# Front of a hybrid decoder layer: three square roots instead of two, GpSimd normalizes the second half, six PSUM banks, other queues for three loads

## What is computed

```python
h = rmsnorm(x, ln1_g)               # xf * rsqrt(mean(xf * xf) + 1e-6) * g
x = x + hybrid_mixer(h, w_in, ...)  # h @ w_in, 8 stick-breaking heads, 4 linear-attention heads, @ w_out
h = rmsnorm(x, ln2_g)
x = x + hierarchical_moe(h, ...)    # 4 groups of 8 experts, top 2 of one group
return rmsnorm(x, ln_f_g)
```

## Time and profile before

| | us |
|---|---|
| median of three runs (lowest, highest) | 1315.86 (1309.72, 1317.32) |
| profiled execution: span from first to last instruction | 1320.3 |
| TensorE matmuls busy | 1214.6 (92%) |
| VectorE busy | 901.6 (68%) |
| ScalarE busy | 741.1 (56%) |
| GpSimd busy | 306.3 (23%) |
| start of the block after the front (first matmul of L568) | 39.68 |

### The profile page before, as it was taken

The page is one execution under the profiler, slowest core; times in us unless marked ns, Lnnn a source line. Parts: engine busy times, 40 slices in busy tenths (PEclk is TensorE's granted clock), DMA queues, the critical chain, the costliest instruction groups (busy, mean ns, idle before and its releaser), DMA issues. The chain is left out here.

```text
span 1320.3 us, 18132 instructions
## 1 busy us (share of the span) xinstructions
PE 1214.6 (92%) x6596; PEld 918.3 (70%) x6596; DVE 901.6 (68%) x844; ACT 741.1 (56%) x760; POOL 306.3 (23%) x273
## 2 busy tenths in 40 slices
PE   3999999998999979799918999999999999999975
PEld 3778787775888768588715777777777777777742
DVE  3365747473474268244657898899888988998816
ACT  5364646463532333311235777877777787778613
POOL 1000000002011011000151444444444444444400
PEclk8999999998999995799958999999999999999989
DMA  5210101001110020452329999999999999999847
GB/s 175 64 33 17 33 17 33 17 17 41 40 33 17 1 96 33 140 202 96 97 92 353 401 392 387 383 384 379 385 392 380 385 378 386 382 387 394 308 165 315
DMA packets 83152, 271.63 MB, mean 206 GB/s; under 512 B 14640, under 2 KB 45472, under 8 KB 58528
## 3 DMA queue, kind: packets, MB, share of 16 engines
q1 hardware_dynamic: 72640, 248.31, 50.5%
q0 software_dynamic: 9312, 18.45, 4.3%
q10 hardware_dynamic: 1152, 4.19, 0.8%
HBM read 253.91 MB, written 25.79 MB: 212 GB/s over the span
## 5 line engine op out<-in xcount | busy, mean ns | idle before, releaser
L1984 PE MATMUL ps<-w_high,in_hi 128*96 128x512 f32 x512 | 204.3, 399 | 4.8 <-DVE hid L1912 2.9
L1984 PE MATMUL ps<-w_lower,in_hi 128*96 128x512 f32 x512 | 202.3, 395 | 0.0
L1984 PE MATMUL ps<-w_high,in_lo 128*96 128x512 f32 x512 | 202.1, 395 | 0.0
L1254 POOL DMA_INDIRECT x_g<-h_dram,who x33 | 155.6, 4716 | 40.5 <-POOL who L1250 27.8
L1926 DVE TENSOR_TENSOR d_lo<-cat,d_hi 128x2048 fp32r<-128x2048 f32 x64 | 146.3, 2287 | 24.5 <-ACT d_hi L1848 22.5
L1898 DVE TENSOR_TENSOR w_lower<-w_raw,w_high 128x2048 fp32r<-128x2048 f32 x62 | 141.7, 2286 | 24.6 <-ACT w_high L1827 24.6
L1903 DVE TENSOR_TENSOR w_lower<-w_raw,w_high 128x2048 fp32r<-128x2048 f32 x64 | 143.4, 2279 | 4.2 <-PEq L1333 4.2
L1848 ACT ACTIVATE d_hi<-cat 128x2048 fp32r<-128x2048 f32 x64 | 122.2, 1911 | 20.0 <-PEq L1333 17.1
L1833 ACT ACTIVATE w_high<-w_raw 128x2048 fp32r<-128x2048 f32 x62 | 118.9, 1919 | 25.3 <-PE ps L1984 15.7
L1827 ACT ACTIVATE w_high<-w_raw 128x2048 fp32r<-128x2048 f32 x62 | 118.3, 1908 | 0.0
L501 DVE TENSOR_TENSOR_SCAN prod<-cat 128x256 f32<-128x256 f32 (+7 forms) x64 | 83.4, 1345 | 41.7 <-ACT cat L429 41.7
(11 more groups left out here) (293 smaller groups left out, 2420.4 us busy)
## 6 DMA issues: line engine op xcount, KB each, us to landing
w_raw<-exp_w_gate SPq DMA_DIRECT2D x64, 1024.0 KB
w_raw<-exp_w_up SPq DMA_DIRECT2D x64, 1024.0 KB
cat<-exp_w_down SPq DMA_DIRECT2D x64, 1024.0 KB
w_raw<-w_in SPq DMA_DIRECT2D x22, 512.0 KB, 3.8
xt<-x SPq DMA_DIRECT2D x8, 512.0 KB, 6.6
w_raw<-w_out SPq DMA_DIRECT2D x8, 512.0 KB, 5.2
x_g<-x SPq DMA_DIRECT2D x8, 512.0 KB, 3.7
x_dram<-cat SPq DMA_DIRECT2D x8, 512.0 KB
```

Of the source, the lines that this page charges most:

```text
L1254: pool.indirect_dma_start(x_g[0:CAP, j, :], None, k["h2_dram"][:, :], bass.IndirectOffsetOnAxis(ap=who[j][0:CAP, 0:1], axis=0), bounds_che ...
L1984: mm = pe.matmul(out, x_[:, n // 3, :], w_[:, n // 3, :], start=(n == 0), stop=(n == 3 * KD - 1))
```

## The change

`BANKS` = 6 replaces the 4 PSUM banks for turning; bank 6 stays with the first query product. The w_in tiles are issued by SP behind x, without waiting. The gains are issued by ScalarE's queue as its first instruction. Roots are taken after two, four and eight tiles; VectorE inverts each. The second half is multiplied by GpSimd. ScalarE takes the first turned group out between squares 5 and 6, and makes w_hi after the fourth group; VectorE makes w_lo after its fourth remainder.

```diff
@@ -203,82 +203,108 @@
     g1 = sb("g1", [P, KD], F32, c)
     x_in = [sem(f"x_in{t}", c) for t in range(NT)]
     g_in = sem("g_in", c)
-    rms_done, xn_done = sem("rms_done", c), sem("xn_done", c)
+    rms_done, inv_done, late_done = sem("rms_done", c), sem("inv_done", c), sem("late_done", c)
+    xn_done = sem("xn_done", c)
     turned, hi_done, lo_done = sem("turned", c), sem("hi_done", c), sem("lo_done", c)
     groups = [(hf, kd) for hf in range(NH) for kd in range(KD)]
     per = NT // NH
-    BANK_Q = 6
+    parts = (slice(0, 2), slice(2, 4), slice(4, NT))
+    BANKS, BANK_Q = 6, 6
     with nc.Block() as block:
         @block.sync
         def _(sp):
             for t in range(NT):
                 sp.dma_start(xt[:, t, :], a["x"][0, t * P:(t + 1) * P, :]).then_inc(x_in[t], 16)
-            with nc.allow_non_contiguous_dma(reason="a thousand gains, features to partitions"):
-                sp.dma_start(g1[:], a["ln1_g"][0].rearrange("(k p) -> p k", p=P)).then_inc(g_in, 16)
+            for j, col in enumerate((COL_SB_Q, COL_SB_K, COL_SB_V)):
+                sp.dma_start(w_raw[:, j], a["w_in"][0, :, col:col + P].rearrange("(k p) c -> p k c", p=P))\
+                  .then_inc(w_first[j], 16)
 
         @block.gpsimd
         def _(pool):
-            for j, col in enumerate((COL_SB_Q, COL_SB_K, COL_SB_V)):
-                for t in range(2 if j == 0 else NT):
-                    pool.wait_ge(x_in[t], 16)
-                pool.dma_start(w_raw[:, j], a["w_in"][0, :, col:col + P].rearrange("(k p) c -> p k c", p=P))\
-                    .then_inc(w_first[j], 16)
+            pool.wait_ge(inv_done, 3)
+            for t in range(per, NT):
+                pool.tensor_scalar(xn[:, t, :], xt[:, t, :], inv[:, t:t + 1], None, ALU.mult).then_inc(late_done, 1)
 
         @block.scalar
         def _(act):
-            A.step(act.activation(spare[:], ones[:, 0:1], ACT.Sqrt))
-            for t in range(NT):
+            def square(t):
                 act.wait_ge(x_in[t], 16)
                 A.step(act.activation(squares[:], xt[:, t, :], ACT.Square, accum_out=ss[:, t:t + 1]))
-                if t % per == per - 1:
-                    part = slice(t + 1 - per, t + 1)
-                    act.activation(rms[:, part], ss[:, part], ACT.Sqrt, bias=k["eps_t"][:], scale=1.0 / D).then_inc(rms_done, 1)
-                if t == per - 1:
-                    act.wait_ge(w_first[0], 16)
-                    act.activation(w_hi[:, 0], w_raw[:, 0], ACT.Copy).then_inc(whi_done, 1)
+
+            def root(m):
+                act.activation(rms[:, parts[m]], ss[:, parts[m]], ACT.Sqrt, bias=k["eps_t"][:],
+                               scale=1.0 / D).then_inc(rms_done, 1)
+
+            def take_hi(n):
+                hf, kd = groups[n]
+                act.wait_ge(turned, n + 1)
+                act.activation(h_hi[:, kd, hf * HALF:(hf + 1) * HALF], bank(k, n % BANKS), ACT.Copy,
+                               scale=g1[:, kd:kd + 1]).then_inc(hi_done, 1)
+
+            with nc.allow_non_contiguous_dma(reason="a thousand gains, features to partitions"):
+                act.dma_start(g1[:], a["ln1_g"][0].rearrange("(k p) -> p k", p=P)).then_inc(g_in, 16)
+            A.step(act.activation(spare[:], ones[:, 0:1], ACT.Sqrt))
+            square(0)
+            square(1)
+            root(0)
+            square(2)
+            square(3)
+            root(1)
+            square(4)
+            square(5)
             act.wait_ge(g_in, 16)
-            for n, (hf, kd) in enumerate(groups):
-                act.wait_ge(turned, n + 1)
-                act.activation(h_hi[:, kd, hf * HALF:(hf + 1) * HALF], bank(k, n % 4), ACT.Copy,
-                               scale=g1[:, kd:kd + 1]).then_inc(hi_done, 1)
+            take_hi(0)
+            square(6)
+            square(7)
+            root(2)
+            for n in range(1, 4):
+                take_hi(n)
+            act.wait_ge(w_first[0], 16)
+            act.activation(w_hi[:, 0], w_raw[:, 0], ACT.Copy).then_inc(whi_done, 1)
+            for n in range(4, 2 * KD):
+                take_hi(n)
 
         @block.vector
         def _(dve):
-            def normalize(hf):
-                part = slice(hf * per, (hf + 1) * per)
-                dve.wait_ge(rms_done, hf + 1)
-                V.step(dve.reciprocal(inv[:, part], rms[:, part]))
-                for t in range(hf * per, (hf + 1) * per):
-                    dve.tensor_scalar(xn[:, t, :], xt[:, t, :], inv[:, t:t + 1], None, ALU.mult).then_inc(xn_done, 1)
+            def invert(m):
+                dve.wait_ge(rms_done, m + 1)
+                dve.reciprocal(inv[:, parts[m]], rms[:, parts[m]]).then_inc(inv_done, 1)
 
             def take_lo(n):
                 hf, kd = groups[n]
                 cols = slice(hf * HALF, (hf + 1) * HALF)
                 dve.wait_ge(hi_done, n + 1)
-                dve.scalar_tensor_tensor(h_lo[:, kd, cols], bank(k, n % 4), g1[:, kd:kd + 1],
+                dve.scalar_tensor_tensor(h_lo[:, kd, cols], bank(k, n % BANKS), g1[:, kd:kd + 1],
                                          h_hi[:, kd, cols].bitcast(F32), ALU.mult,
                                          ALU.subtract).then_inc(lo_done, 1)
 
-            normalize(0)
+            for m in range(2):
+                invert(m)
+                dve.wait_ge(inv_done, m + 1)
+                for t in range(2 * m, 2 * m + 2):
+                    dve.tensor_scalar(xn[:, t, :], xt[:, t, :], inv[:, t:t + 1], None, ALU.mult).then_inc(xn_done, 1)
+            dve.wait_ge(g_in, 16)
+            take_lo(0)
+            invert(2)
+            for n in range(1, 4):
+                take_lo(n)
             dve.wait_ge(whi_done, 1)
             dve.tensor_tensor(w_lo[:, 0], w_raw[:, 0], w_hi[:, 0].bitcast(F32), ALU.subtract).then_inc(wlo_done, 1)
-            dve.wait_ge(g_in, 16)
-            for n in range(KD):
-                take_lo(n)
-            normalize(1)
-            for n in range(KD, 2 * KD):
+            for n in range(4, 2 * KD):
                 take_lo(n)
 
         @block.tensor
         def _(pe):
             def turn(n):
                 hf, kd = groups[n]
-                if kd == 0:
-                    pe.wait_ge(xn_done, per * (hf + 1))
-                if n >= 4:
-                    pe.wait_ge(lo_done, n - 3)
+                if n == 0:
+                    pe.wait_ge(xn_done, per)
+                if n == KD:
+                    pe.wait_ge(late_done, per)
+                if n >= BANKS:
+                    pe.wait_ge(lo_done, n - BANKS + 1)
                 for j in range(per):
-                    mm = pe.transpose(k["ps"][:, n % 4, j * P:(j + 1) * P],
+                    mm = pe.transpose(k["ps"][:, n % BANKS, j * P:(j + 1) * P],
                                       xn[:, hf * per + j, kd * P:(kd + 1) * P], ident[:])
                 mm.then_inc(turned, 1)
```

## The result

The changed kernel takes 1317.78 us (median of 22 runs, 1312.66 to 1320.44) against 1315.01 of the kernel before on the same chip (22 runs, 1309.03 to 1318.61). The ratio is 1.0023 with a 95% interval of 1.0013 to 1.0033, that is 1.7 to 4.3 us slower. Forecast was 6.6 us faster. The profiled execution itself took 1316.76, its span 1315.2.

What follows compares the result with a forecast made beforehand. The front was taken as a chain over several engines, the rest as TensorE's queue. The early start's 1.1, the 5.64 stop and 1.31 wait, less w_lo's cost, gave 6.6 us saved: 1309.3 from the 1315.86 median, range 1302 to 1316.

Steps and rivals of the forecast that it cites:

- GpSimd's price: Second half's normalization: 1.4 us a GpSimd pass, four make 5.6, ready at 23.5, or 24.7 if put back by w_lo.
- Rival 2: Second half: GpSimd becomes the bound at 2.0 to 2.7 a pass, front ends at 33.8 to 37.8 us; chance 0.15.
- rival 1: Gap before the twelve products: TensorE's clock falls, costing 2.4 us, front over at 35.5, whole 1311.7; chance 0.25.
- rival 3: w_lo waits for all four GpSimd passes; at 2.71 each, 1316.8 us; chance of slower 0.05, of smaller-price starving 0.1.
- The gains: Gains loaded ahead of x or between its packets: delay x by 0.3 us at x3, 0.5 by x7.
- The first bank between squares: ScalarE's order: first turn done at 14.3 us, taken out until 15.0, then squares 6 and 7.
- the three roots: Start of the front: a root after two tiles lets turning start at 13.4 instead of 14.48, gaining 1.1 us.
- the queues: Loads: w_in behind x brings x's last tile at 15.0 us before gains, first w_in tile at 17.0, no split wait.
- Six banks: Turning the first half: turns 0 to 5 need no bank freed, done at 18.7 us; all eight at 20.4.
- w_lo beside GpSimd: VectorE's w_lo subtraction waits 0.7 us for the GpSimd pass under way, done at 22.4; a pass put back by 1.2.
- Rival 4: Later stages: the front's gain doesn't arrive, whole gains 0 to 3 us, about 1314.5; chance 0.1.

Runs made afterwards that it cites:

- experiment 1: Changed kernel, but VectorE instead of GpSimd normalizes the second half, right behind w_lo; ratio 0.9972 to the kernel before, front ends at 34.63 us.
- experiment 4: Kernel before, with only GpSimd multiplying the second half and VectorE inverting the second roots ahead of its remainders; ratio 1.0034, front ends at 43.01 us.
- experiment 10: Changed kernel, with GpSimd multiplying by the constant 1.0 instead of the column of inverses; one run, front ends at 40.92 us, passes 2.76 to 2.79.
- experiment 9: Kernel before, unaltered, measured as if new; ratio 1.0000, front ends at 39.13 us.
- experiment 3: Changed kernel, with 28 filler transposes into unused bank 7 between the twelve products and the ninth turn; ratio 1.0012 to the kernel before, front ends at 38.76 us.
- experiment 5: Changed kernel again, unaltered, beside other runs of the kernel before; ratio 1.0024, front ends at 40.69 us.
- experiment 7: Changed kernel with VectorE normalizing the second half, plus 14 filler transposes ahead of the first product; ratio 0.9968 to the kernel before, front ends at 33.62 us.
- experiment 8: Changed kernel with VectorE normalizing the second half and four PSUM banks for turning instead of six; ratio 0.9943 to the kernel before, front ends at 33.83 us.
- experiment 12: Changed kernel, VectorE and GpSimd normalizing two tiles each, w_hi and w_lo before take-outs 1 to 3, gains behind x's sixth tile; ratio 0.9945 to before, front 33.01 us.
- experiment 6: Changed kernel with VectorE normalizing the second half and ScalarE issuing the gains after the first root; ratio 0.9996 to the kernel before, front ends at 37.49 us.
- experiment 2: Changed kernel, with VectorE normalizing two tiles of the second half behind w_lo and GpSimd two; ratio 0.9968 to the kernel before, front ends at 35.12 us.
- experiment 11: Changed kernel with VectorE normalizing the second half, four banks, gains issued between x's sixth and seventh tile; ratio 0.9937 to the kernel before, front ends at 33.58 us.

## Why the prediction was wrong, step by step

**The step that failed is GpSimd's price.** The text put a pass between 0.94 and 2.71 and took 1.4, "nearer the fill since there is one input". It costs 2.83, beyond its ceiling. The bound was wrong in kind: the row of the two-input product has 512 elements, and its cost doubled is a guess, no ceiling; of the two rows it was the one that computes, the fill only writes. The estimate of 1.54 that the prediction set beside it was too low as well. Multiplied by four, 5.7 us lay in that choice, more than in any other miss of the sum. Experiments 1, 4 and 10 show it: taken away, the front is 6.75 shorter; put alone into the kernel before, 3.3 longer (3.9 against experiment 9); and a pass stays at 2.8 without its second operand.

**Rival 2 was the right mechanism at too small a price.** It let the front end at 37.8 at most. To that come 1.1 for GpSimd's later start (18.95 instead of 17.85) and 2.5 for the clock, while the passes took 11.97, as much as the 10.84 with the 1.2 allowed for w_lo: 41.4, as measured. The prediction had rival 1, the clock, only ahead of the products; it did not ask what a TensorE that waits for GpSimd does to its clock. Experiment 3 shows these 2.5 us alone. The range, too, was cut short of the text's own worst case: rival 3 gave 1316.8, and the range ended at 1316.

**Rival 1 came true in this profile as well, at no price.** Eight of the twelve products came 0.43 apart, and they ended at 27.2 instead of 25.2. In experiment 5 they ended at 25.6, and the ninth turn started at 30.93 all the same, since it waited for GpSimd. What was quoted for this rival, that after transposes the products would start at the low clock in any case, did not hold: in experiments 5, 7, 8 and 12 they were fast from the start.

**The gains.** Priced at 0.3 by x3, between 0 and 1.28. Ahead of everything they stop x for about 1.0: the second square starts at 8.40 instead of 7.39. So the start gained 0.3 instead of 1.1, and GpSimd starts 1.1 us later than forecast. Experiment 6 shows the cause. That tiny packets are far fewer bytes was no measure: between 5 and 6 us the DMA engines moved 848 packets and 57 GB/s, three us later 118 packets and 422 GB/s.

```profile
DMA packets 848, 0.06 MB, mean 57 GB/s; under 512 B 835, under 2 KB 835, under 8 KB 848
```

**The first bank between squares, the three roots, the queues.** They did what was worked out, 1 us later: take-out at 15.40 (14.35), root 2 at 18.33 (17.3), no wait for w_in. First products at 22.62 against a forecast of 22.4; the two misses here, 1.0 for the gains and 0.7 for a w_lo that did not wait, cancel.

**Six banks.** Not needed ahead of the products (experiment 8): w_lo ends the wait, so that early turns only leave TensorE idle longer. Behind them they may save 0.35.

**w_lo beside GpSimd.** Costed at 0.7, cost 0 (1.23 against 1.22): it began 0.5 before the pass's end, and the next GpSimd pass was put back by 0.65 instead. Rival 3's starving did not occur, not even where w_lo began within a pass (experiment 12, +0.3). The Trainium skill (SBUF — State Buffer, Who interferes with whom) calls the shared way an exclusive lock, held for the whole instruction, that blocks the loser fully. The earlier trace rows agree with it, experiment 12 does not: by it w_lo would have waited until 21.4, and it ended at 20.7.

**The whole against the front.** The prediction said that a microsecond in the front is one in the whole. Against the first profile of before, front and whole moved as follows:

| experiment | 1 | 2 | 3 | 4 | 6 | 7 | 8 | 11 | 12 |
|---|---|---|---|---|---|---|---|---|---|
| front, us | -5.1 | -4.6 | -0.9 | +3.3 | -2.2 | -6.1 | -5.9 | -6.1 | -6.7 |
| whole, us | -3.7 | -4.2 | +1.6 | +4.5 | -0.5 | -4.2 | -7.5 | -8.3 | -7.2 |

The first six miss by 0.4 to 2.5 us to the slow side, of which 0.55 is the first profile of before being late, and the last three by 0.5 to 2.2 to the fast side. So the whole follows the front in direction (experiment 3 apart) and in rough size, and 2 us between two versions can't be told from these ratios. Why the changed kernel is 3.0 to 3.2 slower by its ratio, with 1.6 (mean of 41.38 and 40.69 less that of 39.68 and 39.13) in the front, is open; 1.6 lies just outside the first interval (1.7 to 4.3) and within the second (1.5 to 4.9). Up to the experts the profiles show no further loss. What the record does show is that executions spread over more than the effect: 7 of the 22 of before took 1312.0 or less, while 20 of the 22 of the changed kernel took 1316.6 or more, and the stretch from the mix to the experts alone varies by 5 us within one kernel. Whether the change shifts that share or chance does, no run here separates. Rival 4, that later stages take a gain back, was not seen: with fronts 5 to 7 us shorter the whole gained 4 to 8.

## What to carry to other kernels

Before work is moved to an engine whose duration for that kind of instruction is not in the trace, measure one such instruction; a bound from another kind of instruction is a guess, and here four of them made the sign. When a faster step lets one engine arrive early and wait, look for what the idling costs it (here TensorE's clock, 2.5 us behind a wait of 3.75, and 1.3 to 2.5 over four profiles) and for banks or buffers that only bring it there sooner. A load of many tiny pieces belongs where nothing waits for its neighbours: 4 KB in 1024 pieces stopped a 4 MB load for a microsecond ahead of it and landed 8.8 us after its issue behind it.

## What the runs showed of the hardware

- GpSimd multiplies 128x1024 float32 by a column in 2.83 us and by a constant in 2.76; VectorE needs 0.75. GpSimd's two-input product costs less an element: 1.29 for 512 (1.35 in the mean).
- GpSimd and VectorE slow each other in more than one way: a pass begun within VectorE's two-input subtraction took 3.48, VectorE's subtraction begun early in a pass took 1.53 instead of 1.22, and two VectorE normalizations beside a pass 2.18 to 2.27 instead of 1.42 (one of the two took 1.5 to 1.6, the other 0.74).
- Transposes keep TensorE's clock at its high level: 28 of them over 3.22 us, and the turn behind them ran at full speed (experiment 3). The Trainium skill (TensorE: Matmul & The Clock Gate, Part 4: PE-mode transpose) says that they do not engage it; here they kept it, and the trace decides. They also bring it: in experiment 1, where TensorE has done nothing but turn, six or seven transposes run in each microsecond from 14 to 17 and eleven in the next, and the turn at 19.75 takes 0.66, ahead of any product.
- When the clock changes its level is not fixed by the instructions: in the changed kernel turning sped up at 19.3 in one profile and at 17.9 in the other, and the products behind the same gap of 1.92 us were slow in one and fast in the other.
